# The tiles of split weights start at six different places modulo 512 bytes

## The reference, cut to what matters

```python
# first block, layer 0: gated linear attention + sparse attention, then a dense FFN
x = x + gate * (hybrid_mixer(modulate(x), w_in[1024 x 2856], ...) @ w_out)
x = x + gate * swiglu(modulate(x), w_gu[1024 x 5632], w_down[2816 x 1024])
# layer 1: Mamba-2 mixer, then 8 experts, top 2 of 8
x = x + gate * mamba2_mixer(modulate(x), w_in[1024 x 5152], ..., w_out[2048 x 1024])
for e in range(8):
    out = out + gate[..., e:e+1] * swiglu(h, w_gu[e][1024 x 7168], w_down[e][3584 x 1024])
# final norm, then twice: two kinds of attention, 8 + 8 heads
proj = h @ w_in_2[l][1024 x 4096];  y = concat(o_a, o_b) @ w_out_2[l][1024 x 1024]
# six times in all: mod = silu(c) @ w_mod[1024 x 3072]
```

## Time and profile before

| | us |
|---|---|
| median of 3 runs | 2073.43 (2073.12 to 2076.48) |
| the profiled execution, its own time | 2075.21 |
| span of its instructions | 2073.4 |
| PE busy | 1975.6 (95%) |
| DVE busy | 1725.3 (83%) |
| ACT busy | 1328.1 (64%) |
| DMA queue q1, share of 16 engines | 74.1% |
| mean granted TensorE clock | 0.982 |

### The profile page before, as it was taken

The page is one execution under the profiler, slowest core; times in us unless marked ns, Lnnn a source line. Parts: engine busy times, 40 slices in busy tenths (PEclk is TensorE's granted clock), DMA queues, the critical chain, the costliest instruction groups (busy, mean ns, idle before and its releaser), DMA issues.

```text
span 2073.4 us, 28446 instructions
## 1 busy us (share of the span) xinstructions
PE 1975.6 (95%) x10316; PEld 1644.3 (79%) x10316; DVE 1725.3 (83%) x2440; ACT 1328.1 (64%) x1977; POOL 0.2 (0%) x4
## 2 busy tenths in 40 slices
PE   6998999989989999999999999999999998999997
PEld 5777889978877788788888878888888876767785
DVE  7798878768776698989989898998989988785764
ACT  4353534355564587788788787888878774554543
POOL 0000000000000000000000000000000000000000
PEclk9999999999999999999999999999999999999999
DMA  9856689846332298999999999999989994672630
GB/s 378 300 170 234 229 301 327 287 142 207 116 111 82 91 382 325 359 334 382 366 351 365 329 368 345 374 352 340 371 325 377 380 354 158 222 247 68 217 122 21
DMA packets 154211, 560.19 MB, mean 270 GB/s; under 512 B 17232, under 2 KB 17488, under 8 KB 153936
## 3 DMA queue, kind: packets, MB, share of 16 engines
q1 hardware_dynamic: 154064, 558.29, 74.1%
HBM read 557.18 MB, written 1.05 MB: 269 GB/s over the span
## 4 chain that ended last, share of the span: by engine, by line
PE 78%; DVE 12%; ACT 5%; issue 3%; DMA 2%; DVEq 0%; SPq 0%; ACTq 0%
PE ps L527 22%; PE ps L529 22%; PE ps L528 22%; PE ps L533 10%; DVE spl L516 3%; PE ps L537 3%; DVE macc L580 2%; ACT sph L504 2%; DMA ring<-in_hyb_w_in 1%; DVE arena L2169 1%; DMA ring<-in_dense_down 1%; ACT arena L771 1%; ACT arena L2135 0%; DVE hL L884 0%; ACT ps L890 0%
## 5 line engine op out<-in xcount | busy, mean ns | idle before, releaser
L504 ACT ACTIVATE sph<-ring 128x1024 fp32r<-128x1024 f32 x906 | 949.2, 1059 | 517.0 <-PE ps L529 332.8
L516 DVE TENSOR_TENSOR spl<-ring,sph 128x1024 fp32r<-128x1024 f32 x906 | 1078.2, 1219 | 241.5 <-ACT sph L504 229.0
L527 PE MATMUL ps<-sph,hH 128*128 128x512 f32 (+1 forms) x1296 | 522.6, 403 | 1.4 <-DVE hL L884 1.3
L529 PE MATMUL ps<-sph,hL 128*128 128x512 f32 (+1 forms) x1296 | 507.8, 392 | 0.0
L528 PE MATMUL ps<-spl,hH 128*128 128x512 f32 (+1 forms) x1296 | 506.9, 391 | 0.0
L529 PEld LDWEIGHTS ps<-sph,hL 128*128 128x128 f32 x1296 | 245.5, 189 | 52.6
L527 PEld LDWEIGHTS ps<-sph,hH 128*128 128x128 f32 x1296 | 246.4, 190 | 51.3 <-issue 3.8
L528 PEld LDWEIGHTS ps<-spl,hH 128*128 128x128 f32 x1296 | 246.4, 190 | 48.4 <-issue 1.0
L527 PE MATMUL ps<-sph,rH 128*128 128x512 f32 x664 | 269.1, 405 | 5.9 <-ACT arena L3123 2.3
L529 PE MATMUL ps<-sph,rL 128*128 128x512 f32 x664 | 259.9, 391 | 0.0
L528 PE MATMUL ps<-spl,rH 128*128 128x512 f32 x664 | 259.4, 391 | 0.0
(11 more groups left out here) (317 smaller groups left out, 1754.4 us busy)
## 6 DMA issues: line engine op xcount, KB each, us to landing
ring<-in_moe_gu SPq DMA_DIRECT2D x448, 512.0 KB, 5.4
ring<-in_moe_down SPq DMA_DIRECT2D x224, 512.0 KB, 5.3
ring<-in_mod SPq DMA_DIRECT2D x144, 512.0 KB, 5.0
ring<-in_w_in SPq DMA_DIRECT2D x64, 512.0 KB, 4.5
ring<-in_dense_gu SPq DMA_DIRECT2D x44, 512.0 KB, 5.3
ring<-in_ssm_w_in SPq DMA_DIRECT2D x40, 512.0 KB, 4.2
ring<-in_dense_down SPq DMA_DIRECT2D x22, 512.0 KB, 5.4
ring<-in_hyb_w_in SPq DMA_DIRECT2D x20, 512.0 KB, 5.9
```

Source lines behind the costliest of these rows:

```text
L504: a.activation(k.high[m % SPLITS][:, 0:w], raw[:, 0:w], ACT.Copy).then_inc(k.S.half_rounded, 1)
L516: v.tensor_tensor(k.low[m % SPLITS][:, 0:w], raw[:, 0:w], k.high[m % SPLITS][:, 0:w], ALU.subtract).then_inc(*k.tick(k.S.half_split, f"hal ...
L527: pe.matmul(out, a[0], b[0], start=start, stop=False, skip_group_check=True)
L529: return pe.matmul(out, a[1], b[0], start=False, stop=stop, skip_group_check=True)
```

## The change

Two lists of six tiles become six pairs, each with a tile of padding ahead of it, and the part of SBUF that is set aside for descriptors of GpSimd's DMA queue shrinks from its default of 16,384 bytes to 1,024 in each partition.

```diff
+LEADS = (16, 32, 64, 80, 96, 112)
...
-        self.high = [sb(f"sph{i}", [128, QUARTER], F32R) for i in range(SPLITS)]
-        self.low = [sb(f"spl{i}", [128, QUARTER], F32R) for i in range(SPLITS)]
+        self.high, self.low = [], []
+        for i, lead in enumerate(LEADS):
+            sb(f"pad{i}", [128, (lead - LEADS[i - 1] if i else lead) % 128])
+            self.high.append(sb(f"sph{i}", [128, QUARTER], F32R))
+            self.low.append(sb(f"spl{i}", [128, QUARTER], F32R))
...
-    nc = _bacc.Bacc("TRN2", target_bir_lowering=False, num_devices=1)
+    nc = _bacc.Bacc("TRN2", target_bir_lowering=False, num_devices=1, dynamic_dma_scratch_size=1024)
```

## The result

The changed kernel is slower. In 9 runs each, its median is 2086.87 us (2082.92 to 2090.38) beside 2075.16 us (2070.05 to 2080.30) of the kernel before on the same chips: a ratio of 1.0058 with a 95% interval of 1.0045 to 1.0072, or 11.7 us more. The profiled execution took 2086.36 us with a span of 2084.5, 11.1 us longer than that of before. The granted clock is the same (0.983 beside 0.982).

What follows compares the result with a forecast made beforehand. PE was taken to bound the kernel through its `mm3` intervals: 7752 matmuls x 4 ns = 31.0 us, x 0.88 = 27 us less, all other terms 0, giving a 2047 us median; own range 2028 to 2062, 8 in 10 2012 to 2097.

Steps and rivals of the forecast that it cites:

- What bounds the kernel: PE, busy for 95% of the span; three `mm3` matmul lines are 66% of the chain that ended last.
- the 13.3 ns: Rest per `mm3` matmul above one column per cycle, 226.7 or 120.0 ns; the only part a new placement can change.
- the value taken for it: Reduction of that rest per `mm3` matmul: 4 ns, chosen between 0.7 and 10.3 ns, giving 31.0 us less of PE.
- in each other's way: SBUF reads of the streaming tile and the next stationary piece collide, beginning at one place modulo 512 bytes.
- item `rest`: 296-column matmuls, every second piece already 160 bytes off: 136.0 ns against 136.7, read as a small gain of 0.7 ns.
- The second rival: Slower: place jumps at every half keep `mm3` matmuls unsettled, 3.3 ns each, 17 us; 2090 to 2096 us, chance 0.26.
- its second half: In the slower case, the 1920 256-column matmuls also lose 3.3 ns each, 6 us more.
- the first rival: The rest per `mm3` matmul is a fixed price of swapping the stationary operand: 0 us change, 2073 us, chance 0.28.
- The forecast of no effect: Trainium skill's rule that weight loads steal no SBUF bandwidth from the running matmul: the change is worth 0 us.
- VectorE, ScalarE, the transfers and the descriptors' room at 0 us: New tile places cost neither engine time, transfers still move whole 4096-byte rows, GpSimd's queue is unused: 0 us each.
- The share on the chain: 0.88 of `mm3` time, 1368 of 1552 us, lies on the critical chain, turning 31.0 us into 27 us.

Runs made afterwards that it cites:

- the uniform kernels: Changed kernel with all six pairs at one place; against the kernel before, ratios 1.0001 at 0 and 64 bytes, 1.0005 at 256, 1.0075 at 128, 1.0089 at 192.
- all_at_0: Changed kernel with all six pairs back at the activations' place, padding behind them, smaller descriptor room kept; ratio to the kernel before 1.0001.
- the kernel in turns: Changed kernel with the pairs at 0 and 192 bytes alternately, so the place jumps at every half; ratio to the kernel before 1.0061.
- all_at_192: Changed kernel with all six pairs 192 bytes past the activations' place; ratio to the kernel before 1.0089.
- the two views at 0 and 64 bytes: Kernel before with pairs unmoved, `hH` and `hL` viewed 64 bytes earlier outside experts and second block; ratios 0.9984 (wrong results), 0.9990 with views consistent.

## Why the prediction was wrong

*What bounds the kernel, and the 13.3 ns* were right: the time is made mostly of the intervals of `mm3`, the pads changed nothing else that shows, and the rest above the columns does depend on the places. What makes up the 13.3 ns was not found.

*The step that failed is the value taken for it*, 4 ns less per matmul, out of "The nearest row speaks for a gain but a small one", and with it the idea that gave it its sign: that the two reads get "in each other's way" because they "all begin at one place". For 512 columns the one place is the best of the seven places modulo 256 that were tried (228.0 ns; the others 229.2 to 233.3). The value rested on item `rest`, where a displacement of 160 bytes cost nothing. That item was no witness. In all the uniform kernels the mean of its 296-column matmuls stays between 136.0 and 137.1 ns, while the 512-column ones go from 228 to 233. Those matmuls never settle in the kernel before either (131 to 140 ns in its trace), where the others do; why was not tested. What I read as a sign that the places hardly matter was a shape that shows little of them. The measured term is 3.3 ns more for 512 columns and 2.0 ns less for 256. One number for both forms was wrong as well: the two differ even in the sign.

*The second rival* had the side, the size (3.3 ns for each 512-column matmul, 17 us, beside 3.3 ns measured) and a row that matters, the settling after transposes. That the 3.3 ns agree is luck, for its mechanism was mostly another. "226.7 is a good state that needs one and the same place everywhere" is refuted by 192 bytes, which keeps one place everywhere and settles at 233.3. The jumps are 0.5 of the 3.3 ns; for the halves at 0 bytes it had them right, as the kernel in turns shows. And its second half, 6 us more from 256 columns, has the wrong sign.

*No effect*, the first rival, is out: all_at_0 and all_at_192 differ in the pads alone, and their ratios are 0.9986 to 1.0015 and 1.0063 to 1.0115. The forecast of no effect, which the prediction also read out of the Trainium skill ("TensorE: Matmul & The Clock Gate", Step-by-step: what each phase is for), falls with it. Whether what the page says, that the next weight load takes nothing from the running matmul, is itself wrong here is not shown, as no run tells which accesses meet. Both operands here are float32r, and that stays a condition of what was measured.

*VectorE, ScalarE, the transfers and the descriptors' room at 0 us* were right, by all_at_0. The waits for landings did not grow, as PE was slower: from 900 to 1700 us, 57.1 + 25.1 us in place of 66.9 + 30.9.

```profile
ACT sph L508 <- DMA ring<-in_moe_gu: 57.1, 162, 1.7
ACT sph L508 <- DMA ring<-in_moe_down: 25.1, 72, 1.9
```

*The share on the chain*, 0.88, was too high as well. With the measured intervals it gives 13.6 us and 11.1 came, so about 0.7 of the change in PE's intervals reached the end. At 128 and 192 bytes the same rule gives 22.6 and 23.2 us and the runs 15.6 and 18.5 (ratios x 2075): again 0.6 to 0.7 of what PE's intervals lost. Part of it can be seen in the experts. From the first `mm3` matmul there to the last, the changed kernel takes 10.8 us more: the settled intervals grew by 14.2 us in total, while the steps from the last matmul of a row to the transposes shrank from 32.2 to 30.1 us, and the rest by 1.3 us. PE waited there for VectorE for 2.2 us before and for 0.2 us after: which fits that a longer row leaves less to wait for. At 192 bytes it is 21.8 us more in the settled intervals and 17.5 in all. Outside the experts the single traces scatter too much to tell.

What stays open is why: whether two reads meet and which, or a read and a write of the next halves, and why 16, 32 and 224 bytes are bad and 64 is nearly good. The runs show the price of each place, not what makes it.

## What to carry to other kernels

When long rows of equal matmuls stand at a constant distance that is above columns over clock, as the 226.7 ns here, that distance can depend on where the moving and the stationary tile begin relative to each other. Scan it with one place for all tiles and one profile each, and read it from starts, before mixing places: a mixture gave little more than the mean of its members. Take the row that stands as a witness from the same shape that carries the time.

## What the runs showed of the hardware

- The interval of float32r matmuls of 512 columns with a new 128 x 128 stationary piece each is 226.7 ns when settled with the pairs 0 or 256 bytes past the activations' tiles (modulo 512), 229.2 at 64 and 233.3 at 192, at a granted clock of 1.00.
- For 256 columns, with the weight tile as the stationary one, the order is another, and, as the two views at 0 and 64 bytes show, it is the relative place that counts: means of 115.3 ns at 64 bytes, 117.4 at 192, 119.0 at 128 and 119.9 at 0.
- At 0 bytes, the intervals need several matmuls to settle after an interruption: 230.0 ns over six in the earlier trace rows, and over all rows of the kernel before some ten intervals until 226.7 is reached. At 192 bytes they are 233.1 ns or more from the second on. The trace of the kernel at 128 bytes shows that a place may have several lasting patterns: 238, 229, 237, 230 ns in turn in some items and a cycle of seven (241, 233, 231, 231, 229, 230, 232) in others.
- VectorE's subtraction (1221 to 1222 ns) and ScalarE's rounding (1060 to 1061) of 1024 columns are the same at both kernels' places.
